# Folding the transforms of s: sums and differences of mirrored tokens, one weight slot for the forward and one for the inverse

## What is computed

```
def hyena_mixer(u, w_in, b_in, conv_w, conv_b, ..., skip, w_out, b_out):
    L = u.shape[1]                                   # 512
    z = short_conv(u @ w_in + b_in, conv_w, conv_b)
    x0, x1, v = jnp.split(z, 3, axis=-1)
    s = (v * x1).astype(jnp.float32)
    g = hyena_filter(L, ...)                         # (2L, D)
    n = 2 * L
    y = jnp.fft.irfft(jnp.fft.rfft(s, n=n, axis=1) * jnp.fft.rfft(g, n=n, axis=0)[None],
                      n=n, axis=1)[:, :L]
    y = (y + s * skip.astype(jnp.float32)).astype(u.dtype) * x0
    return y @ w_out + b_out
```

## Time and profile before

| what | value |
|---|---|
| runs, median (lowest to highest) | 1575.12 us (1574.12 to 1576.87) |
| span of the profiled execution | 1572.3 us |
| median of the runs less that span | 2.8 us |
| PE busy | 1495.1 us, 95% |
| DVE, ACT, POOL busy | 952.0, 572.7, 125.7 us |
| mean granted TensorE clock, share of full | 0.972 |

### The profile page before, as it was taken

How to read it: one execution, slowest core, us unless ns; L and a number is a source line. 1 busy time by engine, 2 the same in 40 slices (tenths; PEclk the granted TensorE clock), 3 DMA queues, 4 the chain that set the end, 5 groups by cost and what they waited for, 6 DMA issues and landing times.

```text
span 1572.3 us, 17974 instructions
## 1 busy us (share of the span) xinstructions
PE 1495.1 (95%) x6732; PEld 1210.7 (77%) x6732; DVE 952.0 (61%) x1215; ACT 572.7 (36%) x740; POOL 125.7 (8%) x117
## 2 busy tenths in 40 slices
PE   6999999879998999999999999999899999999996
PEld 5678667657886888888888778887688888888884
DVE  6776665763554567547637787789766533443346
ACT  4321562441433354323314454543333321321222
POOL 1000131220000000000000110154100000000000
PEclk8899999889999999999999999999999999999998
DMA  5222115114320222223232232234232323222231
GB/s 208 89 75 90 65 54 188 41 54 187 107 81 28 81 80 107 82 106 107 81 108 87 100 108 107 80 126 139 83 107 86 112 97 107 80 107 99 89 107 53
DMA packets 23486, 153.08 MB, mean 97 GB/s; under 512 B 2811, under 2 KB 2955, under 8 KB 7040
## 3 DMA queue, kind: packets, MB, share of 16 engines
q1 hardware_dynamic: 18720, 134.23, 24.1%
q0 software_dynamic: 3984, 15.68, 2.9%
q10 hardware_dynamic: 720, 2.30, 0.4%
HBM read 145.90 MB, written 6.30 MB: 97 GB/s over the span
## 4 chain that ended last, share of the span: by engine, by line
PE 86%; DVE 8%; ACT 3%; issue 2%; DMA 1%; POOL 0%; SPq 0%; DVEq 0%; ACTq 0%; POOLq 0%
PE ps L1359 26%; PE ps L1361 26%; PE ps L1360 26%; DVE w_lo L724 1%; PE ps L1698 1%; DMA raw<-weights_dram 1%; DVE opA_lo L767 1%; PE ps L1539 1%; ACT w_hi L392 1%; PE ps L1590 1%; PE ps L1558 1%; PE ps L1460 1%; PE ps L1685 1%; PE ps L1548 1%; DVE gen L1027 1%
## 5 line engine op out<-in xcount | busy, mean ns | idle before, releaser
L1359 PE MATMUL ps<-opA_hi,w_hi 128*128 128x512 f32 x1184 | 470.4, 397 | 15.3 <-DVE opA_lo L775 11.7
L1361 PE MATMUL ps<-opA_hi,w_lo 128*128 128x512 f32 x1184 | 464.5, 392 | 0.0
L1360 PE MATMUL ps<-opA_lo,w_hi 128*128 128x512 f32 x1184 | 464.5, 392 | 0.0
L392 ACT CAST w_hi<-raw 128x2048 fp32r<-128x2048 f32 x119 | 227.2, 1909 | 386.9 <-PE ps L1361 382.7
L724 DVE TENSOR_TENSOR w_lo<-raw,w_hi 128x2048 fp32r<-128x2048 f32 x119 | 277.8, 2335 | 126.0 <-ACT w_hi L392 125.8
L1359 PEld LDWEIGHTS ps<-opA_hi,w_hi 128*128 128x128 f32 x1184 | 224.8, 190 | 68.3 <-DVE w_lo L724 12.7
L1360 PEld LDWEIGHTS ps<-opA_lo,w_hi 128*128 128x128 f32 x1184 | 224.9, 190 | 47.4 <-issue 1.4
L1361 PEld LDWEIGHTS ps<-opA_hi,w_lo 128*128 128x128 f32 x1184 | 224.4, 190 | 47.8
L1359 PE MATMUL ps<-opB_hi,w_hi 128*128 128x512 f32 x608 | 238.9, 393 | 7.3 <-DVE spec L1251 2.6
L1360 PE MATMUL ps<-opB_lo,w_hi 128*128 128x512 f32 x608 | 238.1, 392 | 0.0
L1361 PE MATMUL ps<-opB_hi,w_lo 128*128 128x512 f32 x608 | 237.9, 391 | 0.0
(11 more groups left out here) (276 smaller groups left out, 1585.0 us busy)
## 6 DMA issues: line engine op xcount, KB each, us to landing
raw<-weights_dram SPq DMA_DIRECT2D x126, 1024.0 KB, 4.8
g_dram<-gen POOLq DMA_DIRECT2D x8, 512.0 KB, 3.6
h<-x_t_dram SPq DMA_DIRECT2D x4, 512.0 KB, 11.1
h<-x_t_dram POOLq DMA_DIRECT2D x1, 2048.0 KB, 12.4
scores<-g_dram POOLq DMA_DIRECT2D x4, 512.0 KB, 3.6
g_spec<-g_dram POOLq DMA_DIRECT2D x4, 512.0 KB, 3.6
out_dram<-h ACTq DMA_DIRECT2D x4, 512.0 KB, 2.7
mem_raw<-mem_t_dram POOLq DMA_DIRECT2D x1, 1024.0 KB, 10.7
```

The lines of the kernel that those rows point to most:

```text
L392: A.copy(w_hi[:, p, :], raw[:, p, :]).then_inc(hi_ready, 1)
L1359: W.matmul(out, w[0], x[0], start=start, stop=False)
L1360: W.matmul(out, w[0], x[1], start=False, stop=False)
L1361: return W.matmul(out, w[1], x[0], start=False, stop=stop)
```

## The change

The sum over 512 tokens is folded. With e(t) = s(t) + s(512-t) and o(t) = s(t) - s(512-t), the cosines of even frequencies and the sines of odd ones see only e, the others only o. So each forward product contracts over 256 rows in place of 512. The tokens 0 and 256 have no mirror, and tiles 0 and 1 of a half correct for them with extra matmuls of one row or with a small table (`nyq`). The inverse gives for each channel tile an "odd" and an "even" output of 256 or 258 tokens side by side in one PSUM bank, and mirrored tokens are put together afterwards.

- POOL folds s (`eo_feat`, two operations of 255 columns and two of one column for each tile) during `hy_in`, before the transposes.
- The forward uses 12 matmuls of 512 columns for a tile, with 8 more for n = 0 and 4 and 2 more for n = 1 and 5. The inverse of a half has the same 96 matmuls, of 256 or 258 columns, and 8 more of 258 columns with one row. The "odd" half of them reads its moving operand backwards.
- The whole forward table sits in slot 0 (`w_hi[:, 0]`), and the whole inverse table (`inv_hi`, `inv_lo`, 2052 columns) in slot 1. Both are loaded and split during the last pairs of `hy_in`. Six pairs, with their splits, go.
- The low part of the imaginary part is made on POOL (`y_lo_im`) and no longer on DVE.
- After an inverse, ACT copies 257 columns from PSUM with a scale (`even_parts`), DVE adds the odd output to the mirrored tokens and to the plain ones (255 columns each) and then adds s times skip (512 columns).
- Buffers move: `w_hi` by 32 bytes, `w_lo` by 64, everything above by 96.

```diff
-SECTIONS += [("hy_in", 12), ("dft_s0", 2), ("dft_s1a", 1), ("idft_0", 2), ("dft_s1b", 1), ("idft_1", 2),
-             ("hy_out", 4)]
+SECTIONS += [("hy_in", 12), ("fold_fwd", 1), ("fold_inv", 1), ("hy_out", 4)]
...
+            for c in range(KT):
+
+                pool.wait_ge(hz_done, c + 1)
+                e, o_, x, back = (eo_feat[:, c, 1:HALF], eo_feat[:, c, HALF + 1:T], s_feat[:, c, 1:HALF], s_feat[:, c, T - 1:HALF:-1])
+                nc.gpsimd.tensor_tensor(e, x, back, ALU.add)
+                nc.gpsimd.tensor_tensor(o_, x, back, ALU.subtract)
...
                 nc.gpsimd.tensor_tensor(t[:, 2, :], t[:, 2, :], t[:, 3, :], ALU.add).then_inc(spec_sum, 1)
+                for i in ([n - 1] if n else []) + ([n] if n == 7 else []):
+
+                    im = 2 * (i % 4) + 1
+                    pool.wait_ge(y_hi, 2 * i + 2)
+                    nc.gpsimd.tensor_tensor(op_lo[0][:, im, :], spec[:, i % 2, 2, :], op_hi[0][:, im, :].bitcast(F32),
+                                            ALU.subtract).then_inc(y_lo_im, 1)
...
+            def even_parts(half):
...
+                    act.wait_ge(inv_done, c + 1)
+                    A.activation(hy_val_feat[:, c % 4, 0:HALF + 1], ps[:, 4 + c % 4, HALF - 1:T], ACT.Copy,
+                                 scale=filter_norm[:, c:c + 1]).then_inc(pn_done, 1)
...
                     dve.wait_ge(y_hi, 2 * n - 2)
-                    dve.wait_ge(y_lo, 2 * n - 2)
+                    dve.wait_ge(y_lo, n - 1)
+                    dve.wait_ge(y_lo_im, n - 1)
...
             def hyena_sums(half):
...
+                for c in range(4 * half, 4 * half + 4):
+                    y, odd = hy_val_feat[:, c % 4, :], ps[:, 4 + c % 4, :]
+                    dve.wait_ge(pn_done, c + 1)
+                    V.scalar_tensor_tensor(y[:, HALF + 1:T], odd[:, 0:HALF - 1], neg_norm[:, c:c + 1], y[:, HALF - 1:0:-1],
+                                           ALU.mult, ALU.add).then_inc(late_half, 1)
...
             def inverse(half):
...
                 for q in range(4):
...
+                    pe.wait_ge(y_lo, 4 * half + q + 1)
+                    pe.wait_ge(y_lo_im, 4 * half + q + 1)
...
+                        if q < 2:
+                            at_e, at_o = EC + q * (HALF + 2), ES + q * HALF
+                            back = slice(at_o + HALF - 1, at_o - 1, -1)
+                            even = ps[:, 4 + c, HALF - 2:T]
+                            W.matmul(odd, y_im[0], inv_hi[:, back], start=q == 0, stop=False, skip_group_check=True)
...
+            pair_ready(F_PAIR)
+            pe.wait_ge(bank_read, 2 * F_PAIR)
+            for n in range(6):
+                forward_s(n)
+            pair_ready(I_PAIR)
+            pe.wait_ge(st_lo, 8)
             inverse(0)
-            forward_s(1, (2, 3), 6)
+            forward_s(6)
+            forward_s(7)
             inverse(1)
```

## The result

| | median (lowest to highest) | span of the profiled execution | its clock |
|---|---|---|---|
| before, beside it | 1574.62 us (1573.32 to 1576.87) | 1572.3 us | 0.972 |
| after | 1589.89 us (1584.69 to 1591.72) | 1582.8 us | 0.965 |

The changed kernel is slower: the ratio is 1.0093, with a 95% interval of 1.0074 to 1.0111. The forecast was 1556 us. The profiled execution of after is its lowest, 1584.69 us, so its trace shows some 5 us less than the median.

A forecast was written before the change was run, and what follows sets the result against it. PE bounds the kernel, but the work between forward and inverse sets the transforms' pace. 23.2 us gained, less 3 for clock and 1 for unpriced links, is 19.2: span 1553.1, with 2.8 around it 1556 us; range 1549 to 1565.

The forecast's parts named there:

- the late part: Unchanged rest of `hy_out`, starting at 1162.76 before; forecast to start at 1139.6, 23.2 us earlier, before deductions.
- Nothing moves up to the products of n = 0: Folds, splits and loads ahead of DVE's first products at 1059.83 cost no time.
- steps 2 to 6: Chain from the products of n = 1 through both inverses into `hy_out`, ending at 1139.6, 23.2 us earlier.
- POOL's link: In the transforms, products of tile n+2 wait for POOL's imaginary low part of tile n: turns of 7.3 to 7.4 us.
- the rival that has them contended throughout: In the transforms, DVE contention lengthens POOL's operations, a sum taking 1.74 us, not 1.30: 1562 to 1563 us; chance 0.14.
- backward operands: Half of the inverse's matmuls, reading backwards, run at half speed, 0.234 us: 1563 to 1564 us; chance 0.06.
- weight loads: In the inverses, weight loads aren't hidden, 0.22 us a matmul: 1570 to 1571 us; chance 0.04.
- POOL's low part 3: POOL's imaginary low part of tile 3, at 1095.3, releases the last quarter of inverse 0, which ends at 1098.4.
- One-row forms: One-row matmuls, not priced; they share 1 us with semaphores and blocked low parts on DVE.
- The 3 us taken off: Clock loss behind PE's gaps in inverse 1 and first `hy_out` chunks: two or so stretches costing 1.7 us each.
- Step 5: ACT, DVE and POOL work between inverse 0 and the last quarter of inverse 1, from 1098.4 to 1123.7.
- steps 5 and 6: From the end of inverse 0 to `hy_out`'s third chunk, which PE may start at 1134.1; two chunks then take 5.4 us.

The follow-up runs named there:

- a_place: Changed kernel with the buffers PE loads weights from in 512-column products back on multiples of 8 KB against the operands: 1569.71 us, ratio 0.9962.
- a_dma: Changed kernel with the forward table loaded over all 128 partitions and partition 0's rows written over it afterwards: 1581.42 us, ratio 1.0032.
- a_both: Changed kernel with high weight buffers at +128 bytes, low ones +256, the rest +288, and the loads of `a_dma`: 1590.28 us, ratio 1.009.
- a_fold: `a_place` with the loads of `a_dma`, so the changed kernel with both edits: 1560.43 us, ratio 0.9904.

## Why the prediction was wrong

Two steps failed. Both are things that the prediction put at nothing, so neither is a term of its sum.

1. **The price 0.227 as a constant.** "From the late part on nothing is changed, and PE is the bound there, so what the late part moves by is what the kernel gains" takes PE's price in the rest of the kernel as unchanged, and "Nothing moves up to the products of n = 0" takes it so ahead of the transforms. The move of the buffers stood in the text only as "the shift of all weight buffers by 32 or 64 bytes under each matmul of the kernel", with part of a chance of 0.04. It is a factor on nearly the whole kernel: 0.0044 us on each 512-column matmul, 20.2 us (`a_place` against after). It decided the sign: without it the ratio is 0.9962.
2. **"Nothing moves up to the products of n = 0".** I gave the loads "a slot's whole turn of 12 us or more", taking their size for their price. The whole table is 1 MB and should take what a pair takes; two of its eight loads had a shape that moves at 26 GB/s. It costs 8.5 to 9.3 us (`a_dma`, `a_both`, `a_fold`, each against the same kernel without the edit), and what I had named as a sign of a wrong prediction, "`hy_in` gets longer than it was", happened.

With both undone, `a_fold` can be held against steps 2 to 6. Times are from the first forward matmul, 1051.69 in the forecast and 1053.56 in `a_fold`, its PE timeline:

```profile
1053.56 0.47 PE L1465 MATMUL ps<-opB_hi,w_hi 128*128 128x512 f32 x1 [0.40 <-issue]
...
1076.29 0.76 PE L1465 MATMUL ps<-opB_hi,w_hi 128*128 128x512 f32 x1 [5.45 <-DVE spec L1355]
1076.85 0.63 PE L1466 MATMUL ps<-opB_lo,w_hi 128*128 128x512 f32 x1
...
1085.52 0.50 PE L1465 MATMUL ps<-opB_hi,w_hi 128*128 128x512 f32 x1
...
1089.28 0.28 PE L1898 MATMUL ps<-inv_hi,opA_hi 128*128 128x256 f32 x1
...
1090.50 0.39 PE L1898 MATMUL ps<-inv_hi,opA_hi 128*128 128x256 f32 x1
...
1091.42 0.38 PE L1909 MATMUL ps<-nyq_inv,opA_hi 1*128 1x258 f32 x1
1091.64 0.27 PE L1910 MATMUL ps<-nyq_inv,opA_lo 1*128 1x258 f32 x1
1091.85 0.39 PE L1898 MATMUL ps<-inv_hi,opA_hi 128*128 128x256 f32 x1
...
1095.33 0.28 PE L1898 MATMUL ps<-inv_hi,opA_hi 128*128 128x256 f32 x1
...
1096.04 0.28 PE L1898 MATMUL ps<-inv_hi,opA_hi 128*128 128x256 f32 x1
...
1102.99 0.28 PE L1467 MATMUL ps<-inv_hi,opA_lo 128*128 128x256 f32 x1
...
1141.44 0.50 PE L1465 MATMUL ps<-opB_hi,w_hi 128*128 128x512 f32 x1 [2.08 <-DVE w_lo L821]
...
1148.63 0.39 PE L1465 MATMUL ps<-opB_hi,w_hi 128*128 128x512 f32 x1
```

Its DVE timeline at the products of n = 2, 3 and 5 and at two contended groups:

```profile
1073.66 0.69 DVE L1352 TENSOR_TENSOR spec<-ps,scores 128x512 f32<-128x512 f32 x1 [0.23 <-DVE opA_lo L864]
...
1080.95 0.69 DVE L1352 TENSOR_TENSOR spec<-ps,g_spec 128x512 f32<-128x512 f32 x1 [4.08 <-POOL opA_lo L450]
...
1097.54 0.69 DVE L1352 TENSOR_TENSOR spec<-ps,g_spec 128x512 f32<-128x512 f32 x1 [4.83 <-POOL opA_lo L450]
...
1112.36 5.71 DVE L1392 TENSOR_TENSOR hy_val_feat<-hy_val_feat,x_feat 128x512 f32<-128x512 f32 x4
1118.00 0.68 DVE L864 TENSOR_TENSOR opA_lo<-spec,opA_hi 128x512 fp32r<-128x512 f32 x1
...
1121.12 5.71 DVE L864 TENSOR_TENSOR opB_lo<-hy_val_feat,opB_hi 128x512 fp32r<-128x512 f32 x4
```

| us behind the first forward matmul | forecast | `a_fold` |
|---|---|---|
| products of n = 2 | 20.2 | 20.1 |
| n = 3 | 27.5 | 27.4 |
| n = 5 | 43.7 | 44.0 |
| end of inverse 0 | 46.7 | 49.7 |
| late part | 87.9, with 4 taken off 91.9 | 95.1 |

- **Right:** POOL's link. DVE waits 4.08 and 4.83 us for POOL's low part, the turn is 7.29 us, and the chain of products is met within 0.3 us up to n = 5. POOL's operations took 1.26 to 1.31 us in these turns, so the rival that has them contended throughout didn't come there.
- **Right:** the inverse's full matmuls. Six in a row, three of 256 columns backwards and three of 258 forwards, take 0.71 us (1095.33 to 1096.04), 0.118 each, and at the lower level (clock 0.50 from 1118 to 1122) 0.213 each. Behind a change of form six take 0.92 (1090.50 to 1091.42, with a change at both ends). So the rivals on backward operands and on weight loads fall. The Trainium skill ("TensorE: Matmul & The Clock Gate", Part 3, The mechanism) has a load overlap a matmul only when its row group differs, though the same section also lets a load into the background weight buffer run ahead. The trace disagrees with the first here as it did before.
- **Mis-sized: inverse 0 ends 3.0 late.** It isn't released by "POOL's low part 3"; PE itself is late. Behind its gap of 5.45 us PE ran nearly all of forward n = 4 at the lower level (clock 0.50 from 1076.3 to 1085.0): its 20 matmuls took 9.2 us (1076.29 to 1085.52), at 0.227 they would take 4.5. Forward 5 began 2.0 late and, with two one-row matmuls in it, took 3.8 in place of 3.2, so it ended at 35.7 instead of 33.2. And a group of six matmuls with two one-row ones takes 1.35 us (1090.50 to 1091.85) where eight at 0.117 are 0.94: 0.4 for each of four groups. "One-row forms" were only in the 1 us for everything unpriced.
- **Mis-sized: contention on DVE.** The four products by x0, and the four low parts behind them, take 5.71 us each where the earlier trace rows gave 4.68, since POOL now has three operations in that time: 2.1 more.
- **Mis-sized: the clock.** Behind its wait of 2.08 us PE ran the last 24 matmuls ahead of the late part in 7.19 us (1141.44 to 1148.63, clock 0.76), where 5.4 were forecast. The 3 us taken off were for such stretches. This one took 1.8, and the one of 4.7 in forward n = 4 reached the chain in part, as above.
- **Mis-sized: the start.** The first forward matmul comes at 1053.56, 1.9 later than before. Of these 1.1 were there at the RECIPROCAL already, where kernels without the fold lie nearly as late (1014.02 to 1014.26). The other 0.8 come between the two (39.24 in place of 38.46), and no run shows why.
- **A slip of the sum.** Step 5 takes 3.7 us for a low part and the products of n = 7, where its own prices give 0.6 + 2.5 = 3.1. They took 3.1 (1118.00 to 1121.12).

Together: PE's last wait ends at 87.9 where steps 5 and 6 give 82.4. Of these 5.5, 3.0 are from inverse 0 and 2.1 from contention on DVE, and the rest are small terms of either sign. With the 1.8 behind that wait the late part is 7.2 behind the chain's 87.9, for which 4 were taken off: 3.2 short. These and the start's 1.9 make up nearly all of the 5.4 us by which the span misses the forecast (1558.5 against 1553.1). The fold alone is worth 13.8 us by the spans and 16.1 by the medians; the forecast was 19.2.

## What to carry to other kernels

Before you trust a table of spared instructions, look at what else the edit touches under every instruction of the kernel: weight buffers moved by 32 and 64 bytes cost 20 us here, more than the whole fold brings. Count matmuls in a stretch without gaps in both traces; a busy share of 100% reads the same when each matmul is slower. Price a DMA by its shape and not by its bytes, since a load of 127 partitions ran at 26 GB/s, a sixteenth of the best rate; load 128 and write the odd row over it.

## What the runs showed of the hardware

- The distance of two 512-column fp32r matmuls with a weight load each depends on where the weights lie against the streaming operands: 0.2267 us for a shift of 0 or 256 bytes, 0.2324 for 128, 0.2333 for 32 or 64 of both weight buffers or 32 of the low one alone, 0.2311 for 64 of the low one alone or 32 and 64. A shift of everything together by 32 does nothing.
- Behind a load of 127 partitions SP took 7.29 and 9.42 us to issue a one-row load; with loads of 128 partitions, and after they have landed, the same one-row loads take 0.56 to 0.71 us to issue. So a slow transfer can hold up the issue of the next, and not only its own data.
- A one-row matmul of 258 columns cost more than a full one: 0.22 us from the first of a pair to the second, against 0.118. The pair and the two changes of form add 0.4 us to a group of eight.
